# Product-key expert layer on one core: 64 gate batches inside the last u blocks, with fewer gathered rows between the searches

## The reference, cut to what matters

```
q = (h @ wq).reshape(B, S, 8, 2, 128)
sub_scores = einsum('bshpk,hpnk->bshpn', q, subkeys)      # 128 first keys, 128 second keys per head
top_v, top_i = top_k(sub_scores, 16)
cand = top_v[..., 0, :, None] + top_v[..., 1, None, :]    # 16 x 16 pairs
best_v, best_pos = top_k(cand, 16)
expert = first key * 128 + second key of the best 16 pairs
gates = softmax(best_v)
hid = gelu(einsum('tkd,td->tk', u[expert], x)) * gates    # 8 heads x 16 experts per token
out = einsum('tk,tkd->td', hid, v[expert])
```

## Time and profile before

| | |
|---|---|
| median of 3 runs | 2865.7 us |
| span of the profiled execution | 2863.0 us |
| what lies around the span, against that median | 2.7 us |
| TensorE busy | 2716.7 us (95%) |
| VectorE busy | 1595.0 us (56%) |
| GpSimd busy | 1362.7 us (48%) |
| ScalarE busy | 937.4 us (33%) |
| first u block starts | 1810.4 |
| last u block ends, hole begins | 2273 |
| v loop | 2349.5 to 2798.2 |
| moved by DMA | 598.85 MB, mean 209 GB/s |

### The profile page before, as it was taken

The page is one execution under the profiler, slowest core; times in us unless marked ns, Lnnn a source line. Parts: engine busy times, 40 slices in busy tenths (PEclk is TensorE's granted clock), DMA queues, the critical chain, the costliest instruction groups (busy, mean ns, idle before and its releaser), DMA issues.

```text
span 2863.0 us, 32244 instructions
## 1 busy us (share of the span) xinstructions
PE 2716.7 (95%) x12062; PEld 2057.0 (72%) x12062; DVE 1595.0 (56%) x3064; ACT 937.4 (33%) x1684; POOL 1362.7 (48%) x1004
## 2 busy tenths in 40 slices
PE   8989999998999899999998789999999999999996
PEld 7856888776888678888777678888888864444442
DVE  1033044476314343440224757999999999756667
ACT  3275343655424333222334433111113670000001
POOL 4432444566446234444352436645446664645445
PEclk9999999999999999999999899999999999999999
DMA  5321233332244136663331035999999849999998
GB/s 164 104 58 30 74 105 92 113 102 70 102 141 145 53 93 194 206 185 123 78 105 38 30 110 205 377 409 408 409 409 385 318 146 409 409 411 409 410 409 327
DMA packets 219373, 598.85 MB, mean 209 GB/s; under 512 B 22337, under 2 KB 47314, under 8 KB 218834
## 3 DMA queue, kind: packets, MB, share of 16 engines
q1 hardware_dynamic: 135280, 300.70, 30.7%
q0 software_dynamic: 75968, 275.81, 24.9%
q10 hardware_dynamic: 7970, 20.28, 2.2%
HBM read 584.84 MB, written 7.41 MB: 207 GB/s over the span
## 4 chain that ended last, share of the span: by engine, by line
PE 72%; DMA 11%; DVE 9%; POOL 3%; ACT 2%; issue 2%; POOLq 0%; DVEq 0%; ACTq 0%; SPq 0%
PE ps L1893 14%; PE ps L1373 14%; PE ps L1374 13%; PE ps L1375 13%; DMA rows<-in_v,expert 6%; DMA rows<-in_u,expert 5%; DVE ps L2597 2%; PE ps L1882 2%; DVE rows L2583 2%; PE ps L1339 1%; POOL wlo L1148 1%; PE ps L1912 1%; PE ps L1472 1%; POOL rows L1279 1%; PE ps L1559 1%
## 5 line engine op out<-in xcount | busy, mean ns | idle before, releaser
L1148 POOL TENSOR_TENSOR wlo<-wraw,whi 128x1024 fp32r<-128x1024 f32 x258 | 627.3, 2442 | 799.5 <-ACT whi L614 709.8
L614 ACT ACTIVATE whi<-wraw 128x1024 fp32r<-128x1024 f32 x258 | 270.0, 1058 | 693.0 <-PE ps L1375 593.4
L1928 PE MATMUL ps<-stream,hg 128*128 128x512 f32 x1024 | 441.7, 594 | 7.8 <-DMA stream<-in_v 7.0
L1893 PE MATMUL ps<-haff,stream 128*128 128x256 f32 x2048 | 445.6, 379 | 2.2 <-ACT stg L1038 2.2
L1373 PE MATMUL ps<-hhi,whi 128*128 128x512 f32 x1088 | 428.4, 394 | 15.6 <-DVE hlo L2059 8.7
L1893 PEld LDWEIGHTS ps<-haff,stream 128*128 128x128 f32 x2048 | 388.0, 190 | 53.8 <-ACT stg L1038 2.4
L1375 PE MATMUL ps<-hhi,wlo 128*128 128x512 f32 x1088 | 425.5, 391 | 0.0
L1374 PE MATMUL ps<-hlo,whi 128*128 128x512 f32 x1088 | 425.3, 391 | 0.0
L1279 POOL DMA_INDIRECT rows<-in_u,expert x256 | 275.6, 1077 | 239.8 <-DVE hid L2583 122.4
L1928 PEld LDWEIGHTS ps<-stream,hg 128*128 128x128 f32 x1024 | 195.2, 191 | 253.6 <-issue 244.8
L2583 DVE CUSTOM_DVE_ANT_0 rows<-rows,h_s 128x1024 f32<-128x1024 f32 x256 | 318.4, 1247 | 83.4 <-DMA rows<-in_u,expert 83.2
(11 more groups left out here) (485 smaller groups left out, 4331.8 us busy)
## 6 DMA issues: line engine op xcount, KB each, us to landing
stream<-in_ut SPq DMA_DIRECT2D x128, 512.0 KB, 6.8
stream<-in_v SPq DMA_DIRECT2D x128, 512.0 KB, 6.8
wraw<-in_w_in SPq DMA_DIRECT2D x96, 512.0 KB, 3.6
wraw<-in_w_ada SPq DMA_DIRECT2D x48, 512.0 KB, 4.1
wraw<-in_w_gu SPq DMA_DIRECT2D x88, 256.0 KB, 3.7
wraw<-in_w_down SPq DMA_DIRECT2D x22, 512.0 KB, 3.5
decs<-acs_kept ACTq DMA_DIRECT2D x16, 512.0 KB, 3.6
wraw<-in_w_br_ssm SPq DMA_DIRECT2D x16, 512.0 KB, 3.5
```

Source lines behind the costliest of these rows:

```text
L614: act.activation(whi[:, n % WSLOTS, 0:kn, :], wraw[:, n % WSLOTS, 0:kn, :], ACT.Copy).then_inc(w_hi, 1)
L1148: pool.tensor_tensor(wlo[:, n % WSLOTS, 0:kn, :], wraw[:, n % WSLOTS, 0:kn, :], whi[:, n % WSLOTS, 0:kn, :].bitcast(F32), ALU.subtract).th ...
L1893: ins = pe.matmul(ps[:, n % 2, 0:ND], stream[j][:, k, :], haff2[:, 1, k, :], start=k == 0, stop=k == KD - 1)
L1928: ins = pe.matmul(ps[:, 2 * i + half, :], hg[:, n, P * i:P * i + P], stream[j][:, 4 * half:4 * half + 4, :], start=n == 0, stop=n == NKEYS ...
```

## The change

All 64 gate batches are now made behind u blocks 64 to 127, one behind each (`AHEAD` = 64). The hole and its 16 TensorE rows are gone, and VectorE uses these rows. For that the dense searches come early, directly behind those of tile 0, and `WOVEN` gives the places that get a row: 4 in a search of tile 0, 3 in one of tiles 2 and 3, 8 in one of tile 1. All 8 searches of tile 1 come in blocks 15 to 18. The gates are scaled after row 82, the first one-hots follow after row 96, and batch b is made after row 98 + 9 b // 4. The second-key one-hots go from VectorE (one instruction per batch) to ScalarE (four Squares and one Relu of 512 columns); VectorE makes two first-key one-hots instead of one, ScalarE one instead of two. When batch b is mixed, only 65 + b of the 128 blocks have their Gelu in `hg`: these are multiplied, and the gates of the others are copied to `hg`; `late_mix` multiplies them later, over 4 more tokens from block to block, so Gelus of late blocks split at a growing column. The memset of `hg` on GpSimd goes. The lists of loads and Gelus are new.

```diff
-TOP_AFTER = {**{b: b + 1 for b in range(3, 12)}, **{b: b - 2 for b in range(15, 18)}}
-AHEAD = 20
+TOP_AFTER = {b: b - 3 for b in range(15, 19)}
+WOVEN = {0: (1, 3, 5, 7), 2: (1, 4, 7), 3: (1, 4, 7), 1: range(8)}
+AHEAD = ND // 4
 AHEAD_FROM = NKEYS + 1 - AHEAD
-AHEAD_ROW = 199
-MIX_AFTER = divmod(AHEAD_ROW + 2 * (AHEAD - 1), TOPK)
-HOT_DVE, HOT_ACT, HOT_POOL = (0,), (1, 2), (3,)
-GELU_AT = {4: 0, 21: 1, 30: 2, 49: 3, 69: 4, 88: 5, 110: 6, 117: 7}
-HOLE = TOPK * MIX_AFTER[0] + MIX_AFTER[1] + 1
-PE_HOLE = [divmod(HOLE + r, TOPK) for r in range(TOPK)]
+AHEAD_ROW = 98
+HOT_DVE, HOT_ACT, HOT_POOL = (0, 1), (2,), (3,)
+GELU_AT = {4: 0, 17: 1, 50: 2, 66: 3, 81: 4, 95: 5, 109: 6, 116: 7}
+GATES_AT = AHEAD_ROW - 16
+LOADS = {26: (0, 1), **{28 + 6 * q: (q,) for q in range(2, 8)}, 248: (8, 9), 266: (10,), 282: (11,)}
...
+def batch_row(b):
+    return AHEAD_ROW + 9 * b // 4
+
+
+def late_tokens(n):
+    return 4 * (n - AHEAD_FROM + 1)
...
-                mine = hot1_of(b)
+                first, second = hot1_of(b), hot2_of(b)
+                for m in range(4):
+                    c = 4 * b + m
+                    act.activation(second[:, m, :], cst[:, C_IOTA:C_IOTA + P], ACT.Square, bias=slot_k[:, c:c + 1])
                 for m in HOT_ACT:
                     c = 4 * b + m
-                    ins = act.activation(mine[:, m, :], cst[:, C_IOTA:C_IOTA + P], ACT.Square, bias=slot_n[:, 1, c:c + 1])
+                    ins = act.activation(first[:, m, :], cst[:, C_IOTA:C_IOTA + P], ACT.Square, bias=slot_n[:, 1, c:c + 1])
                 link(ins)
+                act.activation(second.rearrange("p m n -> p (m n)"), second.rearrange("p m n -> p (m n)"), ACT.Relu, bias=1.0, scale=-1.0)
...
-                    act.activation(ps[:, n % 2, 0:NA], ps[:, n % 2, 0:NA], ACT.Gelu)
-                    act.activation(hg[:, n, NA:ND], ps[:, n % 2, NA:ND], ACT.Gelu).then_inc(s("hg_ready"), 1)
+                    late = late_tokens(n)
+                    act.activation(ps[:, n % 2, 0:late], ps[:, n % 2, 0:late], ACT.Gelu)
+                    act.activation(hg[:, n, late:ND], ps[:, n % 2, late:ND], ACT.Gelu).then_inc(s("hg_ready"), 1)
...
-                if n == 98:
+                if n == AHEAD_FROM - 5:
                     act.wait_ge(s("head_done"), top_done(3, PEER_HEADS - 1))
...
-                if q >= 9:
-                    pool.wait_ge(s("mix_mm"), ND // 4)
-                tk_s = tk_dense if q < 9 else tk_last
+                if q >= 8:
+                    pool.wait_ge(s("u_mm"), NKEYS)
+                tk_s = tk_dense if q < 8 else tk_last
...
-                    pe.wait_ge(s("late_mixed"), n - AHEAD_FROM)
+                    pe.wait_ge(s("late_mixed"), n - AHEAD_FROM - 1)
...
             pe.wait_ge(s("hg_ready"), NKEYS)
-            pe.wait_ge(s("late_mixed"), 1 + NKEYS - AHEAD_FROM)
-            for b in range(AHEAD, ND // 4):
-                gate_batch(b)
-                if b in HOLE_HALF:
-                    ins = row_half(HOLE_HALF[b] // 2, HOLE_HALF[b] % 2)
-                    if HOLE_HALF[b] % 2:
-                        ins.then_inc(s("pe_row_used"), 1)
+            pe.wait_ge(s("late_mixed"), NKEYS - AHEAD_FROM)
             pe.wait_ge(s("mixed"), ND // 4)
...
+                places = [0]
+
                 def beside(ins):
 
                     steps[0] += 1
                     mine = steps[0]
                     ins.then_inc(dve_step, 1)
-                    between()
+                    if places[0] in WOVEN[t]:
+                        between()
+                    places[0] += 1
                     v.wait_ge(dve_step, mine)
...
-                v.tensor_tensor(hot2_of(b), cst[:, C_IOTA:C_IOTA + P].unsqueeze(1).to_broadcast([P, 4, P]),
-                                ps[:, 3, 4 * b:4 * b + 4].unsqueeze(2).to_broadcast([P, 4, P]), ALU.is_equal)
...
             def mix(b):
 
+                now = AHEAD_FROM + b
+                v.wait_ge(s("hg_ready"), now)
                 v.wait_ge(s("mix_mm"), b + 1)
-                view = hg[:, :, 4 * b:4 * b + 4]
-                v.tensor_tensor(view, view, ps[:, gate_bank(b), :].rearrange("p (m n) -> p n m", m=4), ALU.mult).then_inc(s("mixed"), 1)
+                gates = ps[:, gate_bank(b), :].rearrange("p (m n) -> p n m", m=4)
+                if now < NKEYS:
+                    v.tensor_copy(hg[:, now:NKEYS, 4 * b:4 * b + 4], gates[:, now:NKEYS, :])
+                view = hg[:, 0:now, 4 * b:4 * b + 4]
+                v.tensor_tensor(view, view, gates[:, 0:now, :], ALU.mult).then_inc(s("mixed"), 1)
...
             for h in range(2, PEER_HEADS):
                 top_keys(0, h, between=next_row)
+            for t, h in TOP_ORDER[PEER_HEADS:3 * PEER_HEADS]:
+                top_keys(t, h, between=next_row)
```

More of the change, by code:

```diff
@@ L91 @@
 ENDS = (0, 2, 3, 1)
-NA = 4 * AHEAD
-HOLE_HALF = {AHEAD + 3 + 5 * x // 4: x for x in range(2 * TOPK)}
-HOLE_DIAG = {AHEAD + 4 + 5 * (2 * r + 1) // 4: r + DIAGS for r in range(TOPK - DIAGS)}
-HOLE_NEXT = [AHEAD + 7 + 5 * (2 * r + 1) // 4 for r in range(14)]
+def batch_row(b):
+    return AHEAD_ROW + 9 * b // 4
+def late_tokens(n):
+    return 4 * (n - AHEAD_FROM + 1)
 C_IDENT, C_NEGGE, C_NEGONE, C_LE, C_GT, C_ONE = (P * i for i in range(6))
@@ L1116, in scalar_program @@
                     hots(n - AHEAD_FROM + 2)
-            for b in range(AHEAD, ND // 4):
-                hots(b)
-                if b == AHEAD:
-                    row_diags(PE_HOLE[:DIAGS])
-            for h in range(len(GELU_AT), PEER_HEADS):
-                row_gelu(0, h)
             for h in range(PEER_HEADS):
@@ L1307, in gpsimd_program @@
                     gather_next()
+            hot_before = {batch_row(b) + RING - 4: b for b in range(AHEAD)}
             for b in range(len(BLOCKS)):
                 for k in range(TOPK):
-                    n = TOPK * b + k - (AHEAD_ROW + RING - 4)
-                    if n == 0:
-                        pool.wait_ge(s("head_done"), top_done(*TOP_ORDER[2 * TOP_AFTER[11] + 1]))
-                        pool.memset(hg[:, AHEAD_FROM:NKEYS, 0:NA], 1.0).then_inc(s("late_mixed"), 1)
-                        pool.wait_ge(s("slots_ready"), 1)
-                    if n % 2 == 0 and 0 <= n // 2 < AHEAD + 2:
-                        first_hot(n // 2)
-                    if TOPK * b + k == HOLE + RING:
-                        for m in range(AHEAD + 2, ND // 4):
-                            first_hot(m)
-                            if m in HOLE_NEXT:
-                                gather_next()
-                        load_scores(9)
-                        load_scores(10)
-                    if k == RING and b == 2:
-                        load_scores(0)
-                        load_scores(1)
-                    if k == RING:
-                        if b - 1 in TOP_AFTER and TOP_AFTER[b - 1] < 11:
-                            q = TOP_AFTER[b - 1] - 4 + 2
-                            load_scores(q)
-                        if b - 2 == 15:
-                            load_scores(TOP_AFTER[b - 2] - 2)
-                    if TOPK * b + k == gathered[0]:
+                    r = TOPK * b + k
+                    for q in LOADS.get(r, ()):
+                        load_scores(q)
+                    if r in hot_before:
+                        if hot_before[r] == 0:
+                            pool.wait_ge(s("slots_ready"), 1)
+                        first_hot(hot_before[r])
+                    if r == gathered[0]:
                         gather_next()
@@ L1930, in tensor_program @@
                 ins.then_inc(s("v_mm"), 1)
-            for r in range(len(PE_HOLE), len(PE_ROWS)):
+            for r in range(len(PE_ROWS)):
                 ins = row_half(r, 0)
@@ L2696, in later_weights @@
                 head_weights(*BLOCKS[b][1:]).then_inc(s("wrow_ready"), 1)
-            def gate_matrices():
-                later_weights(PE_HOLE[-1][0])
-                v.wait_ge(s("hg_ready"), NKEYS)
-                hots(AHEAD)
-                for m in range(AHEAD, ND // 4):
-                    if m + 1 < ND // 4:
-                        hots(m + 1)
-                    mix(m)
-                    if m in HOLE_DIAG:
-                        hole_diagonal(HOLE_DIAG[m])
-                v.wait_ge(s("pe_row_used"), TOPK)
-            between_rows = {**{divmod(AHEAD_ROW + 2 * b, TOPK): partial(batch_ahead, b) for b in range(AHEAD)}, divmod(AHEAD_ROW - 2, TOPK): first_ahead,
+            between_rows = {**{divmod(batch_row(b), TOPK): partial(batch_ahead, b) for b in range(AHEAD)}, divmod(GATES_AT, TOPK): scale_gates, divmod(AHEAD_ROW - 2, TOPK): first_ahead,
                             (26, 15): lambda: later_weights(29), (27, 15): lambda: later_weights(30),
@@ L2745, in vector_program @@
                     link(v.tensor_copy(h2_s[:, 0, :], own_sums(0)))
-                    link(v.tensor_tensor(h2_s[:, 0, :], h2_s[:, 0, :], row_sums(1), ALU.add))
             link(add_tile(1, own_sums(1)))
```

43 lines of the change are left out of this document (13 added, 30 removed).

## The result

The changed kernel takes **2892.85 us** (median of 4 runs, 2890.88 to 2896.09) beside 2866.3 for the kernel before on the same chip (4 runs, 2865.52 to 2867.83): ratio **1.0094**, 95% interval 1.0079 to 1.0108. It is slower, as forecast, but by twice as much: the span grew from 2863.0 to 2889.1, so by 26.1 us, where the forecast had 13.2.

A forecast was written before the change was run, and what follows sets the result against it. Bound by the time the DMA engines run without full load while rows remain; sixteen rows (20.5 us) less a 7.3 us earlier search gave +13.2 on the 2863.0 span, 2876.2, so about 2879 us; range 2862 to 2899.

The forecast's parts named there:

- Step 1, the searches: Dense searches: six of tile 0 end at 1843.8 us, then sixteen with three rows each end at 2023.2 us.
- Step 2, the waits: Before the first gate batch: TensorE waits 11 us, then 9 us; first batch done at 2058.8 us.
- rival A: TensorE never waits, if the dense searches end by 2002 us: 2846 us, faster; chance 0.08.
- rival B: Smaller waits: empty places cost nothing (12 us), a row Gelu costs 0.87 us (5.4); 2862 us, no change; chance 0.16.
- Step 3, the pace: Gate batches: TensorE paces at 4.345 us each, five row Gelus add 9.8 us; v loop starts at 2343.4 us.
- the clock's term: After TensorE's idle the clock is lower: some 2 us, charged once on the second wait, bounds 0 and 4 us.
- rival D: ScalarE becomes the pace if its activations do not overlap: about 4.6 us a batch, +16 us, 2895 us; chance 0.10.
- Step 4, the end: After the last batch: tile 1's first search 7.3 us earlier, sixteen rows cost 20.5 us; end +13.2 us.
- the delay of the load of scores: The score load of tile 1's first search waits for the last u block (2341.4 us), issued 0.6 us later.
- its time to land: The score load of tile 1's first search lands in 4.5 us, at 2346.5 us.
- the price of a row: One 524 KB transfer at 409 GB/s, 1.28 us for every row behind; sixteen rows are 20.5 us.
- Rival C: VectorE becomes the pace of the batches if product and copy cost 0.60 us each: +24 us, 2903 us; chance 0.12.

The follow-up runs named there:

- e1: The changed kernel with the row Exps of heads 3 to 7 of tile 0 made beside the dense Exp: 2876.95 us, ratio 1.0041.
- e2: The changed kernel with the scores of tile 1's first search loaded at row 200 into their own buffer: 2888.07 us, ratio 1.0075.
- e6: The changed kernel with the edits of e1 and e2, batches from row 84 on and 155 rows to 64 batches: 2870.89 us, ratio 1.0016.
- e9: The changed kernel with an unused Exp over 16 columns behind five more u blocks: 2895.4 us, ratio 1.0096.

## Why the prediction was right in sign and half in size

*What bounds the kernel*: in line with the table. The Trainium skill has two statements on the rate. Beside the one that the prediction weighed, Perfetto Trace Analysis, "Roofline", says that a core whose neighbour is idle can exceed 358 GB/s and is bounded by its DMA engines at about 435. The windows agree with this one: 409 and 410 GB/s from 2500 to 2790 in the two kernels.

*Step 1, the searches*: they began at 1840.7 instead of 1843.8 and took 10.9 us each instead of 11.05, since only about half of the 8.6 us of stretched instructions came back. The end was near 2017, 6 us before the forecast's 2023.2. 

*Step 2, the waits*: 4.06 and 10.87 us where the forecast had 11 and 9. The first is shorter by the 6 us of step 1. The second is longer, since rows 83 to 96 are wanted in any case, and two of them waited for their DMA (1.85 and 1.01 us). The first batch was done at 2056.2, forecast 2058.8. Both waits were there and at their place, so rival A fell. Of rival B a part came true, since the waits were 14.9 us together and not 20; its other part, a row Gelu at 0.87, did not.

*Step 3, the pace*: 4.345 us for an undisturbed batch was exact, and 2.04 for a row Gelu was near the 1.95. **The step that failed is the clock's term.** I charged it once, 2.0 us on the first batch, and took the short stalls as free of it. The trace has 0.9 us in the first batch (1.84 to the next u block instead of 0.89), 1.5 more in the u block behind it (5.08 for 3.62), and 1.76 three times behind stalls of 1.88 us. So from the first batch done to the last one done there are 291.3 us and not 283.5, and the last was done at 2347.5, 5.2 late; the 7.8 lost here are in part hidden by the 2.6 that steps 1 and 2 were early, which was luck. The transfers ran at 370 GB/s from 2060 to 2340, where I had near 390. e1 is the proof: with the stalls the slow blocks went, and the batches to the v loop lost 15.8 us. How many of the stalls have a slow block behind them varies from profile to profile (last section), so the term can be given only as a range: 0 to 5.3 us in the five profiles with such stalls. Part of rival D is in this, ScalarE as the pace, though in five batches and not in all.

*Step 4, the end*: **three terms were too small**, the delay of the load of scores, its time to land and the price of a row. (The v loop started 6.4 us late, not 5.2, because VectorE was at two rows until 2348.7 when the last batch was done.) The load of scores was issued 1.4 us later behind the last batch, at 2348.6 with GpSimd's gathers ahead of it, and the search began 6.9 behind its issue instead of 4.5. Thus row 240's search was not 7.3 us earlier but 1.7 later; 9.0 us in all (5.2 of step 3, 1.4 and 2.4). e2, which does without this wait, took 4.8 off the median. And sixteen rows cost 24.4 us and not 20.5. Of the 3.9 too little, 1.7 is in the tail, where 16 more v rows by VectorE alone stand 1.39 us apart, as the earlier trace rows had it, and not 1.28. The other 2.2 go with a DMA rate of 402 instead of 409 from 2360 to 2500 (140 x 7 / 409 = 2.4), behind the late scores. These two are read from windows and timelines and were not tried by an experiment. The count of bytes above puts 4.6 us behind 2790, so only their sum of 3.9 is sure, not the split.

The sum: 13.2 + 9.0 + 1.7 + 2.2 = 26.1, in which the last term is what was left over.

*Rival C*, VectorE as the pace, did not occur in the changed kernel: one batch of 64 was 0.25 us longer. It occurred in e6, at 2.42 rows a batch. The range (2862 to 2899) held the measurement.

## What to carry to other kernels

Where one queue of transfers sets the end, count bytes: sum what the DMA engines move up to the end of the stretch, in both kernels, and price a batch, a search or a row by what it takes from that sum. Filling a hole at its place was worth nothing here, where what filled it was taken from a stretch that was full. And when work goes from a stretch where an engine waits to one where it paces, each short stall there has a price that it did not have: look at what stands ahead of the hand-over (the table load behind it in e9 cost nothing), and move Exps next to one another first, which was worth 16 of the 26 us here.
